# Two-layer decoder step on one core: in the sample attention, the mask product opens the score bank, and the scalar engine evicts three of the four key banks

## The reference

```python
def sparse_attend(q, k_sel, v_sel, valid):
    s = jnp.einsum('qhd,qshd->qhs', q.astype(F32), k_sel.astype(F32)) * ATTN_HEAD_DIM ** -0.5
    p = jax.nn.softmax(jnp.where(valid[:, None, :], s, -jnp.inf), axis=-1)
    return jnp.einsum('qhs,qshd->qhd', p, v_sel.astype(F32)).astype(q.dtype)
```

## Time and profile before

| | |
|---|---|
| median of 3 runs | 1239.7 us (1238.57 to 1240.75) |
| the profiled execution | 1238.49 us, of which the span of the core's instructions is 1236.8 us |
| TensorE (PE) busy | 1104.4 us, 89% of the span |
| VectorE (DVE) busy | 584.9 us, 47% |
| ScalarE (ACT) busy | 329.1 us, 27% |
| mean granted TensorE clock | 0.93 of full speed |
| DMA | 319.71 MB, 258 GB/s over the span |

### The profile page before, as it was taken

One profiled execution on the slowest core, in us unless ns is written; L12 is line 12 of the kernel. 1 busy time (PEld: TensorE's weight loads), 2 busy tenths in 40 slices (PEclk: granted clock), 3 DMA queues, 4 the chain that ended last, 5 costly groups with the idle time before them and its releaser, 6 DMA issues.

```text
span 1236.8 us, 14283 instructions
## 1 busy us (share of the span) xinstructions
PE 1104.4 (89%) x5410; PEld 662.1 (54%) x5410; DVE 584.9 (47%) x1113; ACT 329.1 (27%) x520; POOL 42.5 (3%) x77
## 2 busy tenths in 40 slices
PE   3999989779779999898799999999898799998992
PEld 2877656444544343433588865555776634343430
DVE  2667487461622332223876435576753512223325
ACT  3234435330411111112244322314531311111111
POOL 3000000000000000000000001011000000000000
PEclk8899986998789999999699999999999699999996
DMA  9223462385529999988133466898537589999961
GB/s 304 82 98 140 146 251 99 110 306 197 238 100 429 427 427 430 427 353 326 37 136 136 136 221 226 302 351 295 203 132 287 227 346 428 427 430 427 412 246 43
DMA packets 62793, 319.71 MB, mean 258 GB/s; under 512 B 4930, under 2 KB 4962, under 8 KB 50322
## 3 DMA queue, kind: packets, MB, share of 16 engines
q1 hardware_dynamic: 54290, 288.93, 59.3%
q0 software_dynamic: 8160, 28.80, 6.3%
q10 hardware_dynamic: 288, 1.23, 0.3%
HBM read 296.05 MB, written 22.89 MB: 258 GB/s over the span
## 4 chain that ended last, share of the span: by engine, by line
PE 76%; DVE 10%; DMA 9%; issue 2%; ACT 2%; SPq 0%; DVEq 0%; POOL 0%; ACTq 0%; POOLq 0%
PE bank L1105 29%; PE bank L944 16%; PE bank L973 7%; DMA ring<-in_w_exp_up 7%; PE bank L911 4%; PE bank L1362 2%; PE bank L1202 1%; PE bank L923 1%; PE bank L1081 1%; DMA ring<-in_w_in_attn 1%; PE bank L1229 1%; PE bank L1352 1%; PE bank L924 1%; PE bank L1377 1%; DVE Xt L2224 1%
## 5 line engine op out<-in xcount | busy, mean ns | idle before, releaser
L1105 PE MATMUL bank<-ring_parts,XTt_parts 128*128 128x512 f32 (+1 forms) x624 | 201.3, 402 | 7.7 <-DVE ring_parts L2060 7.1
L1105 PE MATMUL bank<-ring_parts 128*128 128x512 f32 x616 | 197.3, 397 | 0.0
L944 PE MATMUL bank<-ring,XTt 128*64 128x512 f32 x768 | 169.5, 598 | 12.8 <-DMA ring<-in_w_exp_up 10.8
L1105 PEld LDWEIGHTS bank<-ring_parts,XTt_parts 128*128 128x128 f32 x624 | 118.6, 194 | 39.5 <-issue 14.9
L1105 PEld LDWEIGHTS bank<-ring_parts 128*128 128x128 f32 x616 | 118.3, 193 | 26.1 <-issue 1.5
L944 PEld LDWEIGHTS bank<-ring,XTt 128*64 128x64 f32 x768 | 56.9, 138 | 122.4 <-issue 106.4
L1890 DVE TENSOR_TENSOR arena<-XTt,bank 128x512 f32<-128x512 f32 x16 | 17.1, 1072 | 210.2 <-PE bank L944 210.2
L973 PE MATMUL bank<-ring,arena 128*64 128x512 f32 x512 | 116.5, 608 | 0.0
L666 DVE TENSOR_TENSOR ring_parts<-ring,ring_parts 128x4096 fp32r<-128x4096 f32 x22 | 97.2, 4420 | 29.6 <-ACT ring_parts L661 29.4
L661 ACT ACTIVATE ring_parts<-ring 128x4096 fp32r<-128x4096 f32 (+1 forms) x24 | 83.3, 3476 | 13.9 <-DMA ring<-in_w_in_ret 6.9
L1515 ACT ACTIVATE arena<-bank 128x512 f32<-128x512 f32 (+6 forms) x123 | 56.4, 485 | 97.4 <-PE bank L1105 57.8
(11 more groups left out here) (256 smaller groups left out, 1279.5 us busy)
## 6 DMA issues: line engine op xcount, KB each, us to landing
ring<-in_w_exp_down SPq DMA_DIRECT2D x32, 2048.0 KB, 13.2
ring<-in_w_exp_up SPq DMA_DIRECT2D x32, 2048.0 KB, 16.0
ring<-in_w_exp_gate SPq DMA_DIRECT2D x16, 2048.0 KB, 12.5
arena<-in_w_exp_gate SPq DMA_DIRECT2D x16, 2048.0 KB, 17.7
ring<-in_w_in_ret SPq DMA_DIRECT2D x12, 2048.0 KB, 9.6
ring<-in_state_ret SPq DMA_DIRECT2D x16, 1024.0 KB, 6.8
out_state_s<-ring POOLq DMA_DIRECT2D x16, 1024.0 KB, 6.6
ring<-in_w_in_attn SPq DMA_DIRECT2D x7, 2048.0 KB, 8.4
```

The costliest lines, as they stand in the source:

```text
L944: last = pe.matmul(ps[64 * j:64 * j + 64, :], xs[:, k, x0:x0 + 64], w[:, k, :], start=(k == 0), stop=(k == KC - 1))
L1105: last = pe.matmul(ps[:, 0:width], x(t, a, k), w[c][:, k, 0:width], **at)
```

## The change

The mask product is issued first, as soon as `qb_ready` is up, and opens the bank; the eight score products are added to it, and the last of them reports the bank full. The waits for the copied key banks now stand behind the mask product. Of the four key banks ScalarE copies 0, 1 and 2, and VectorE copies only bank 3.

```diff
@@ -1257,17 +1257,17 @@
                 if s < NSEQ:
                     ps = fill(("sattn", s))
+                    pe.wait_ge(qb_ready, s + 1)
+                    pe.matmul(ps[:, 0:KEYS], rept[0:64, s % 2, :], bias_s[0:64, :], start=True, stop=False)
                     if s == 0:
                         pe.wait_ge(new_kt, 1)
                     for j in range(4):
                         wait_emptied(pe, "kturn", s, j)
-                    pe.wait_ge(qb_ready, s + 1)
                     for i in range(2):
                         for g in range(4):
                             c, own = 2 * g + i, slice(32 * g, 32 * g + 32)
-                            pe.matmul(ps[own, 0:KEYS], QB[:, c, own], KT[:, c, :], start=(i == 0), stop=False)
-
-                    pe.matmul(ps[:, 0:KEYS], rept[0:64, s % 2, :], bias_s[0:64, :], start=False, stop=True).then_inc(full(("sattn", s)), 1)
+                            last = pe.matmul(ps[own, 0:KEYS], QB[:, c, own], KT[:, c, :], start=False, stop=(i == 1))
+                    last.then_inc(full(("sattn", s)), 1)
@@ -1626,7 +1626,7 @@
-                    for j in range(2):
+                    for j in range(3):
                         ps = wait_full(act, "kturn", s, j)
                         copy(KT[:, 2 * j:2 * j + 2, 0:PAST], ps[:, :].rearrange("p (c k) -> p c k", c=2)).then_inc(freed(("kturn", s, j)), 1)
@@ -2160,9 +2160,8 @@
                     last.then_inc(qb_ready, 1)
-                    for j in range(2, 4):
-                        ps = wait_full(dve, "kturn", s, j)
-                        dve.tensor_copy(KT[:, 2 * j:2 * j + 2, 0:PAST], ps[:, :].rearrange("p (c k) -> p c k", c=2)).then_inc(freed(("kturn", s, j)), 1)
+                    ps = wait_full(dve, "kturn", s, 3)
+                    dve.tensor_copy(KT[:, 6:8, 0:PAST], ps[:, :].rearrange("p (c k) -> p c k", c=2)).then_inc(freed(("kturn", s, 3)), 1)
```

## The result

The changed kernel takes 1229.65 us in the median of 6 executions (1225.61 to 1231.21), the kernel before 1239.03 (1235.09 to 1240.75, 6 executions). The ratio is 0.9924 with a 95% interval of 0.9906 to 0.9942: 7.2 to 11.6 us less. Timed again later, it took 1228.04 against 1239.39, a ratio of 0.9915 (0.9895 to 0.9936). The forecast was 1229.3 us.

The account below looks back on a forecast made before the run. VectorE, with what TensorE does after it, was taken to bound the loop; seven periods at 1.36 us (9.5) plus 0.9 in the first step made 10.4 off 1239.7, so 1229.3 us, range 1225.8 to 1232.5.

Parts of the forecast that it names:

- What bounds the loop: Sample attention loop: VectorE and what TensorE does after it set the 7.11 us step; TensorE idles 1.19 before the scores.
- The mask product: On TensorE in front of the scores: moved into the idle gap, it takes its 0.75 us off each step's chain.
- The copy: Key bank 2 from VectorE to ScalarE: score products can start at 258.36 rather than 258.97 us.
- ScalarE's cover: The third key copy on ScalarE fits a gap, ending 0.12 us before the turned probabilities are due, and costs nothing.
- The sum of a step: One loop step: 5.75 us by VectorE, 5.67 by TensorE; so 5.75 instead of 7.11, 1.36 less.
- The first step: First loop step, where VectorE waits for banks 2 and 3: row maximum at 225.54 instead of 226.47 us, 0.9 less.
- The loop: Whole sample attention loop: seven periods give 9.5 us and the first step 0.9, together 10.4 us less.
- The total: Whole kernel: 10.4 us off the earlier median of 1239.7, giving 1229.3 us.
- Down to the end: After the loop: expert weight loads move forward with TensorE's products, 10.4 us earlier, so no loss was counted.
- a wait for the last end at each change of width: Rival on TensorE: scores start 0.22 us later in each of 8 steps; gain 8.6, time 1231.1 us; 13%.
- The full clock at the loop's end: Rival: the clock holds in the last values and output projection, 3.4 us more; gain 13.8, time 1225.9 us; 8%.
- The overlap of the score products: Rival: score column groups run one after another, 4.5 instead of 1.28 us; about 1254 us in all; 4%.

Follow-up runs that it names:

- a free VectorE: The changed kernel with all four key copies on ScalarE and none on VectorE; step stayed at 5.71 us, time 1228.07 us (ratio 0.9893).
- a mask product at half the price: The changed kernel with the mask product's operands in a float type that takes one pass instead of two; step 5.69 us, time 1229.38 us.
- the kernel with keys turned first: One-pass mask and early VectorE queries, plus TensorE turning the next sequence's keys before the value products; step 6.81 us, time 1234.41 us (ratio 0.9962).

## Why the prediction was right

- *What bounds the loop:* right. VectorE's path with what follows it on TensorE set 7.11 us; each part alone shortened just that path. TensorE's idle time in front of the score products, 9.7 us over the loop before, is 0.1 after.
- *The mask product:* forecast at 0.75 us of a step, 0.82 alone. The 0.07 more agree with the gap from the end of VectorE's copy to the first score product. It is 0.24 before and in the kernel with the copy alone, where the wait for `qb_ready` stands behind those for the key banks, and 0.14 to 0.15 where it stands in front of them, also in the kernel without any mask product. So the gap goes with the order of the waits and not with the product; a kernel in which only this wait moves was not run.
- *The copy:* forecast at 0.61 of a step, 0.60 alone. ScalarE's cover held: 0.12 were predicted between its third copy and the turned probabilities, 0.17 were there.
- *The sum of a step:* 5.75 forecast, 5.71 measured. The term that was off is the one that binds. The prediction had VectorE at 5.75 and TensorE at 5.67; measured alone, VectorE's loop is 5.70 (no mask), TensorE's 5.71 (all copies on ScalarE). VectorE's had been costed with the old gap, 0.24 for 0.14, and with 1.28 for the score products, which stand for 1.32 on that kernel's chain when they end it. TensorE's had 0.11 from the last transpose to the mask product, where 253.89 to 254.10 are 0.21; against that, scores and values hold it 0.03 less each than was put. That 5.75 came so near 5.71 is thus partly luck: it was the sum of the engine that no longer leads, with a gap that no longer holds.
- *The first step:* 0.9 forecast. From the first key transpose to the first row maximum it was 226.47 - 221.31 = 5.16 and became 228.62 - 224.43 = 4.19, where 228.62 is the first maximum of after: 0.97 less. The first of the seven periods is shorter than the others in both kernels, as no value products stand in it, but it fell from 6.13 to 4.72 us, by 1.41, so that seven times the step's gain still holds.
- *The loop:* 10.4 forecast, 10.6 measured at equal clock.
- *The total:* 1229.3 forecast, 1229.65 measured. The forecast took off 10.4 from 1239.7, a median of three; the median of six is 1239.03, and the gain of the medians is 9.4 in the first timing and 11.4 in the second. With executions of one program from 1225.61 to 1231.21, an agreement within 0.4 us is luck; the step and the loop are what was forecast well.
- *Down to the end:* right. From the output projection on, the program took 955.97 and 953.00 us in the two profiles of the changed kernel, against 954.32, so nothing near 10 us was given back. With the clock as before at the loop's end the whole execution was 11.0 shorter. The SP queue's waits for the experts' products after the change are those of before to a few us:

```profile
SPq L703 <- PE bank L944: 124.2, 13, 39.5
SPq L703 <- PE bank L973: 86.0, 7, 14.8
```

- *The rivals:* a wait for the last end at each change of width did not come. It would have started the scores 0.22 later, a step of 5.97 us, and the step is 5.71. The mask's row also ends 0.07 after the scores start (254.10 + 0.80 against 254.83), though the ends are modelled. What the mask product's other shape costs is 0.1 us in front of it (0.21 where transposes go 0.11 apart) and 0.19 of its own 0.73. The Trainium skill has the rule, in "TensorEngine Tiling (Array Packing)", section Key Properties, that changing the tiling mode drains TensorE; this case's trace does not agree if a drain means a wait for the last end. The full clock at the loop's end came in one of two profiles of the changed kernel, so 8% was too low for a single execution; how much of its 3.4 us a median holds is not known from these runs. The overlap of the score products was kept (1.28 for 16 passes), and ScalarE's third copy ended before the turned probabilities came.

## What to carry to other kernels

Before a change that shortens one engine's path, write the loop of every engine as a sum from its rows: the shortest loop one can reach is the second longest of them, and here two came out within 0.01 us of each other, so that neither of two further cuts (a free VectorE, a mask product at half the price) gave anything alone. Work that needs nothing from a late engine belongs in front of the wait for it, on an engine that keeps its program's order; and what stands behind a wait has to be checked for what had covered it, as the kernel with keys turned first shows. Where other stages move the total by a few us from run to run, read a loop's change by its period.

## What the runs showed of the hardware

- The group of score products, 32 columns of the array each, holds TensorE for 1.10 us when products of the same width follow and for 1.22 when transposes 128 wide follow.
- A two-pass mask product alone holds TensorE for 0.73 us between groups of another shape, a second one directly behind it adds 0.54.
- From the end of VectorE's copy to the first product that waits for it there are 0.24 us where one more wait stands behind that for the copy, and 0.14 to 0.15 where none does.
- The clock fell to 1.2 GHz at the end of the loop in one profiled execution of the changed kernel and not in another (269.93 to 272.80 against 271.97 to 273.53 for the same 24 value passes).
